# Preparing each delta unit inside the levels of the one before, quarter-chunk filling, and the eight branch gates in a row

## The reference

```python
q = l2_normalize(heads(q)); k = l2_normalize(heads(k)); v = heads(v)
beta = sigmoid(b_in); g = -exp(a_log) * softplus(a_in + dt_bias)
# chunked gated delta rule, 8 heads of 128
decay = exp(where(causal, g[:, None] - g[None, :], -inf))
lower = where(strict, (k*beta @ k.T) * decay, 0)
sol   = triangular_solve(lower + I, [v*beta, k*beta*exp(g)])
intra = (q @ k.T) * decay
...
o = rms_norm(o, norm_w) * silu(z)
y_d = o @ w_dn_out
...
merged = g_a * y_a + g_c * y_c + g_d * y_d
return x + merged @ w_out
```

## Time and profile before

| | |
|---|---|
| median of 3 runs | 2815.61 us (2809.57 to 2818.78) |
| time of the profiled execution | 2811.89 us |
| its span in the profile | 2809.7 us |
| TensorE matmul busy | 2582.6 us, 92% |
| VectorE, ScalarE, GpSimd busy | 44%, 45%, 53% |
| delta units, layer 0 | 380 to 614 us |
| branch gates, layer 0 | from 614 us |

### The profile page before, as it was taken

One profiled execution on the slowest core, in us unless ns is written; L12 is line 12 of the kernel. 1 busy time (PEld: TensorE's weight loads), 2 busy tenths in 40 slices (PEclk: granted clock), 3 DMA queues, 4 the chain that ended last, 5 costly groups with the idle time before them and its releaser, 6 DMA issues.

```text
span 2809.7 us, 42096 instructions
## 1 busy us (share of the span) xinstructions
PE 2582.6 (92%) x16608; PEld 2213.4 (79%) x16608; DVE 1235.8 (44%) x2156; ACT 1266.2 (45%) x2102; POOL 1479.2 (53%) x857
## 2 busy tenths in 40 slices
PE   6998999989899898988989999998999999898997
PEld 6986878879898687887856776776788868688997
DVE  7782743432677273444347532215000126735323
ACT  5455943344545684434453431234233344434543
POOL 6873754337886476343633122564455546373880
PEclk9998999999999899999999999999999999999999
DMA  5442333244444233334331111223222232134554
GB/s 218 180 150 105 119 138 134 106 150 166 179 168 149 97 129 135 132 124 154 139 131 60 46 61 60 75 90 120 79 91 90 93 117 106 61 120 165 180 185 145
DMA packets 50551, 347.62 MB, mean 124 GB/s; under 512 B 5312, under 2 KB 8640, under 8 KB 8896
## 3 DMA queue, kind: packets, MB, share of 16 engines
q1 hardware_dynamic: 47840, 340.31, 33.5%
q10 hardware_dynamic: 2528, 4.72, 0.5%
HBM read 343.96 MB, written 1.05 MB: 123 GB/s over the span
## 4 chain that ended last, share of the span: by engine, by line
PE 78%; DVE 10%; ACT 6%; issue 2%; POOL 1%; DMA 1%; SPq 0%; ACTq 0%; POOLq 0%; DVEq 0%
PE pg L1706 20%; PE pg L1707 19%; PE pg L1708 19%; PE pg L1731 2%; PE ps L1958 2%; PE ps L1846 2%; PE ps L1966 2%; PE ps L1964 1%; DMA ring<-in_w_stream_dram 1%; ACT ring_hi L708 1%; PE ps L2101 1%; PE ps L1827 1%; POOL ring_lo L601 1%; PE ps L2173 1%; PE ps L2082 1%
## 5 line engine op out<-in xcount | busy, mean ns | idle before, releaser
L601 POOL TENSOR_TENSOR ring_lo<-ring,ring_hi 128x1024 fp32r<-128x1024 f32 (+3 forms) x500 | 1169.9, 2353 | 879.8 <-ACT ring_hi L708 879.1
L1706 PE MATMUL pg<-HH,ring_hi 128*128 128x256 f32 (+1 forms) x3360 | 1075.0, 320 | 32.3 <-DVE HL L1201 10.8
L1707 PE MATMUL pg<-HH,ring_lo 128*128 128x256 f32 (+1 forms) x3360 | 1035.2, 308 | 0.0
L1708 PE MATMUL pg<-HL,ring_hi 128*128 128x256 f32 (+1 forms) x3104 | 961.9, 310 | 0.0
L1706 PEld LDWEIGHTS pg<-HH,ring_hi 128*128 128x128 f32 x3360 | 647.5, 193 | 104.7 <-issue 43.0
L1707 PEld LDWEIGHTS pg<-HH,ring_lo 128*128 128x128 f32 x3360 | 648.2, 193 | 38.9 <-issue 10.6
L1708 PEld LDWEIGHTS pg<-HL,ring_hi 128*128 128x128 f32 x3104 | 598.2, 193 | 30.9
L708 ACT ACTIVATE ring_hi<-ring 128x1024 fp32r<-128x1024 f32 (+6 forms) x564 | 556.5, 1002 | 40.8 <-DMA ring<-in_w_stream_dram 29.6
L718 ACT ACTIVATE take<-pg 128x256 f32<-128x256 f32 (+1 forms) x284 | 120.4, 424 | 532.3 <-PE pg L1708 480.8
L1708 PE MATMUL pg<-big_r,ring_hi 128*128 128x256 f32 (+1 forms) x864 | 276.6, 320 | 0.0
L1706 PE MATMUL pg<-big_r,ring_hi 128*128 128x256 f32 (+1 forms) x736 | 242.3, 329 | 9.3 <-DVE big_r L1646 3.1
(11 more groups left out here) (285 smaller groups left out, 3409.8 us busy)
## 6 DMA issues: line engine op xcount, KB each, us to landing
ring<-in_w_stream_dram SPq DMA_DIRECT2D x320, 1024.0 KB, 4.8
hn<-in_consts_dram ACTq DMA_DIRECT2D x2, 1024.0 KB, 5.6
cst<-in_consts_dram SPq DMA_DIRECT2D x1, 1472.0 KB, 19.8
prm<-in_params_dram SPq DMA_DIRECT2D x1, 1110.0 KB, 7.5
X<-in_xT_dram SPq DMA_DIRECT2D x1, 1024.0 KB, 5.8
X<-in_ctxT_dram ACTq DMA_DIRECT2D x1, 1024.0 KB, 7.9
out_dram<-H ACTq DMA_DIRECT2D x1, 1024.0 KB, 4.8
cst<-in_consts_dram SPq DMA_DIRECT2D x1, 768.0 KB, 16.8
```

The costliest lines, as they stand in the source:

```text
L601: pool.tensor_tensor(ring_lo[:, slot, cols], ring[:, slot, cols], ring_hi[:, place * P:(place + n) * P].bitcast(F32), SUB).then_inc(sem(LO ...
L1706: first = pe.matmul(out, a[0], b[0], start=start, stop=False)
L1707: pe.matmul(out, a[1], b[0], start=False, stop=False)
L1708: return first, pe.matmul(out, a[0], b[1], start=False, stop=stop)
```

## The change

- **Units.** The four preparing products of unit u+1, and what VectorE and ScalarE do with them, move into levels 2 to 5 of unit u. All four go one after the other through `ps` bank 0 (unit 0 still uses four banks). `DT`, `LT`, `IN`, `TT`, `QG` and `EXR` get second buffers. The four exps (and the one of `EXR`) of unit u+1 stand on ScalarE behind the second gap of level 2. The turn of the inverse stands behind the last state product of unit u. The keys are turned at level 6, so only four scalings stand between the values' turn and the next product. Two products move to other banks.
- **Filling.** A chunk or row is cut into quarters. The gaps are new, `dz` comes ahead of `az`, and 12.1 of 82.4 gap units lie ahead of unit 0 (`DELTA_START`).
- **Rows.** The row ahead of the attention's head norm runs as a whole before it, and its turn behind the first `dz` chunk. In `delta_gates` the turn moves from right behind its row to behind the small projection.
- **Branch gates.** The eight gate chunks run in a row, with the modulation row after two of them and its turn after three; they are drained into a buffer `DGATE`, the first of them on ScalarE ahead of `hn_root`. Then come the eight odd chunks, and the filter's steps stand one to two chunks apart instead of two to four.

```diff
-GAPS = [0.8, 5, 0.8] + [1, 1.5] * 5 + [0.6, 2, 0.64, 1, 0.8]
+GAPS = [0.4, 1.0] + [1.9, 0.3] * 4 + [1.9, 0.7] + [1.6, 1.1, 1.0, 0.2]
+LAST_GAPS = [0.4, 1.0] + [1.9, 1.0] * 4 + [1.9, 0.7] + [1.6, 1.1, 1.0, 0.9]
+DELTA_START = [4.3, 7.8]
-    return {"modt": 1}.get(name, 2)
+    return {"modt": 1}.get(name, 4)
...
+def branch_gates(l):
+
+    gates = [("d_out", l, i) for i in range(0, 2 * KD, 2)]
+    row, turn = mods(l, "do")
+    return gates[:2] + [row] + gates[2:3] + [turn] + gates[3:]
...
-        FILTER_1 = [0, 4, 8, 12, 14]
+        FILTER_1 = [0, 2, 4, 6, 7]
```

The preparing products, a new function of TensorE (the other two steps, k·k and k·q, wait for `d_lb` and `d_lt`):

```diff
+            def delta_pre(l, u, step):
+
+                i = 4 * l + u
+                dst = ps[:, 0 if u else step, :]
+                if step == 0:
+                    pe.wait_ge(sem("d_ugib"), i + 1)
...
+                if step == 1:
+                    if u:
+                        pe.wait_ge(sem("d_dt"), i + 1)
+                        pe.wait_ge(sem("d_exr"), i + 1)
```

TensorE, level v of unit u, and the last state product:

```diff
                         ins = pe.matmul(ps[:, 1, s], LM[v % 2][:, s], TM[:, s], start=True, stop=True)
                     ins.then_inc(sem("d_x"), 1)
+                    if 2 <= v <= 5 and u < UNITS - 1:
+                        delta_pre(l, u + 1, v - 2)
+                    if v == 6:
...
+                            ins = pe.transpose(ps[:, 0, s], kT(h, c), ident)
+                        ins.then_inc(sem("d_kt"), 1)
                     fill(next(gaps))
...
                     pe.wait_ge(sem("d_xs"), 6 * i + v)
...
                 ins.then_inc(sem("d_v1"), 1)
+                if u < UNITS - 1:
+                    delta_turn(l, u + 1)
                 fill(next(gaps))
```

VectorE, level s of unit u (n is the next unit):

```diff
+                    if n:
+                        if s == 1 and u:
+                            diagonals(l, n)
+                        if s == 2:
+                            pre_decay(l, n)
+                        if s == 3:
+                            pre_beta(l, n)
+                        if s == 4:
+                            pre_keys(l, n)
+                        if s == 5:
+                            pre_inverse(l, n)
+                            pre_queries(l, n)
+                        if s == 6:
+                            dve.wait_ge(sem("d_x"), 6 * i + 5)
+                            level(l, n, 1)
+                            pre_grown(l, n)
+                    if s == 6:
+                        turned_keys(l, u)
```

ScalarE in unit u, and behind the units:

```diff
                 for s in range(1, 7):
                     fill()
                     act.wait_ge(sem("d_x"), 6 * i + s)
                     act.activation(XS, ps[:, 1, :], ACT.Copy).then_inc(sem("d_xs"), 1)
                     fill()
+                    if s == 2 and u < UNITS - 1:
+                        delta_exps(l, u + 1)
...
                 hn_square(DN[:, 0:8, :])
+                gates = branch_gates(l)
+                drain_fill(gates[:1])
                 hn_root(HN_BASE1(l) + DO_N, 2048, 1.0 / P)
-                drain_fill([("d_out", l, 0)])
-                drain_fill(mods(l, "do"))
+                drain_fill(gates[1:6])
```

TensorE around the units:

```diff
-                fill([("part", mods(l, "att")[0])])
+                fill(mods(l, "att"))
                 head_norm(HN_BASE1(l) + ATT_N, 2048)
-                fill(mods(l, "att"))
+                fill(delta_fill(l)[0])
+                for step in range(4):
+                    delta_pre(l, 0, step)
+                fill(delta_fill(l)[1])
+                delta_turn(l, 0)
                 for u in range(UNITS):
                     delta(l, u)
-                fill([("d_out", l, 0)])
+                gates = branch_gates(l)
+                fill(gates[:1])
                 head_norm(HN_BASE1(l) + DO_N, 2048)
-                fill(mods(l, "do"))
-                for i in range(2 * KD):
+                fill(gates[1:])
+                for m in range(KD):
+                    fill([("d_out", l, 2 * m + 1)])
```

More of the change, by code:

```diff
@@ L211, in delta_fill @@
         parts += [("part", x)] * (n_parts(x[0]) - 1) + [x]
-    gaps = [1.08] + (GAPS * UNITS)[1:]
+    parts.insert(4, parts.pop(0))
+    gaps = DELTA_START + GAPS * (UNITS - 1) + LAST_GAPS
     out = [[] for _ in gaps]
@@ L248, in chunk_order @@
         add("dn", 0, 24)
-        add("cz", 0, EARLY_CZ // 2)
-        out += mods(l, "gates")
-        add("cz", EARLY_CZ // 2, EARLY_CZ)
+        row, turn = mods(l, "gates")
+        add("cz", 0, 2)
+        out.append(row)
+        add("cz", 2, 3)
+        out.append(turn)
+        add("cz", 3, EARLY_CZ)
         out += sum(att_fill(l), []) + mods(l, "att") + whole(sum(delta_fill(l), []))
-        add("d_out", 0, 1)
-        out += mods(l, "do")
-        add("d_out", 1, 16)
+        out += branch_gates(l) + [("d_out", l, i) for i in range(1, 2 * KD, 2)]
         add("w_out", 0, 8)
@@ L739, in drain_fill @@
                         drain(CHUNK[name, l, i], CV[:, i, :], ACT.Silu)
+                    elif name == "d_out" and i % 2 == 0:
+                        drain(CHUNK[name, l, i], DGATE[:, i // 2, :], ACT.Sigmoid)
                     elif name in ("cz", "az"):
@@ L865, in delta_gates @@
                 act.activation(EXA, PR("dn_a_log", l * HEADS, HEADS), ACT.Exp).then_inc(sem("exp_a"), 1)
[L866 to L869, removed]
+                row, turn = mods(l, "gates")
+                drain_fill([("cz", l, 1), row, ("cz", l, 2), turn, ("cz", l, 3)])
                 act.wait_ge(sem("abs_a"), l + 1)
@@ L1905, in delta_gates @@
                 head_norm(HN_BASE1(l) + DK_N, 2048)
-                fill([("cz", l, m) for m in range(1, EARLY_CZ // 2)] + mods(l, "gates"))
-                fill([("cz", l, 2)])
+                row, turn = mods(l, "gates")
+                fill([("cz", l, 1), row, ("cz", l, 2)])
                 pe.wait_ge(sem("hn_done"), HN_BASE1(l) + DK_N + 1)
@@ L1925, in delta, with delta_turn @@
+            def delta_turn(l, u):
+                i = 4 * l + u
+                pe.wait_ge(sem("d_tt"), i + 1)
+                if u == 0:
+                    pe.wait_ge(sem("d_exr"), i + 1)
+                for h, c, s in delta_pair(u):
+                    ins = pe.transpose(ps[:, 0, s], TTS[u % 2][:, s], ident)
+                ins.then_inc(sem("d_t0"), 1)
             def delta(l, u):
                 i = 4 * l + u
-                pair = [(2 * u + p // 2, p % 2, slice(p * P, (p + 1) * P)) for p in range(4)]
@@ L1945, in delta @@
-                fill(next(gaps))
-                pe.wait_ge(sem("d_tt"), i + 1)
-                for h, c, s in pair:
-                    ins = pe.transpose(ps[:, 0, s], TT[:, s], ident)
-                ins.then_inc(sem("d_t0"), 1)
+                pair = delta_pair(u)
+                TT, IN, QG = TTS[u % 2], INS[u % 2], QGS[u % 2]
+                gaps = unit_gaps(l, u)
                 for v in range(1, 7):
@@ L1968, in delta @@
                 for h, c, s in pair:
-                    pe.transpose(ps[:, 0, s], kT(h, c), ident)
-                for h, c, s in pair:
                     ins = pe.transpose(ps[:, 1, s], vT(h, c), ident)
-                ins.then_inc(sem("d_kv"), 1)
+                ins.then_inc(sem("d_vt"), 1)
                 fill(next(gaps))
```

223 lines of the change are left out of this document (139 added, 84 removed).

## The result

| | before | after |
|---|---|---|
| median | 2817.2 us (4 runs, 2809.57 to 2823.7) | **2741.75 us** (4 runs, 2739.5 to 2745.33) |
| ratio to before | | 0.9734, 95% interval 0.9706 to 0.9762 |
| profiled execution, its span | 2811.89, 2809.7 us | 2739.78, 2737.8 us |

The change makes the kernel 2.7% faster. The profiled executions differ by 72.1 us. Three marks on TensorE cut each layer: the attention's head norm, the first gate chunk behind the last unit, and the norm behind `w_out`.

What follows compares the result with a forecast made beforehand. TensorE, busy 92% of the span, bounds the kernel. Gains of 31.5 us per layer, twice 63, less 2 for the filter, give 61: 2751 us for the profiled execution, 2755 us as median; range 2728 to 2790 us.

Steps and rivals of the forecast that it cites:

- The inverse's turn: In the units, the three waits at line 1948 go because preparation starts a unit earlier: 8.2 us gained per layer.
- The clock: In the stretch of the units, slow time behind removed waits comes back: 7 of 7.5 us per layer.
- The other waits in the levels: In the units, 9.6 us of other waits per layer become 8 (5 kept, 3 for exps): gain 1.6 us.
- the 3 us for the exps: In level 3, X's copy stands behind the next unit's exps: 1 us of wait in each of three units.
- all is hidden: Rival: no wait left in the levels or the filter, 3.5 us in the delta gates: 2731 us, chance 0.08.
- Ahead of unit 0: Before the attention's head norm, waits for squares and the row's drain shrink, 1.3 us staying: gain 4.4 us per layer.
- Branch gates: Behind the last unit, the turn waits 0.8 us, not 6.25: 6.5 us idle gained, 3 us more from the clock.
- The worst case: In the branch gates, if gate 4's split lands late, 3 us stay.
- Delta gates: The turn's wait of 3.51 us shrinks to 2.7 for GpSimd's split of `cz` 2: gain 0.8 us per layer.
- The filter: In layer 1 alone, closer steps have less cover and wait: a loss of 2 us, range 0 to 9.
- the signs of being wrong: Waits over 1 us at level 3's second products, filter steps or gates' low parts; level waits above 17 us per layer.
- VectorE behind GpSimd: Rival: three masks in level 5 each meet a split, lasting 2.1 us longer: 2779 us; chance 0.17 with another rival.

Runs made afterwards that it cites:

- the doses: The changed kernel with three, or one, further unused exponentials on ScalarE behind each prepared unit's exps: 2756.26 us with three, 2746.06 us with one.
- the early split: The changed kernel with ScalarE and GpSimd making the splits due at `cz` 1 right behind `cz` 0, in the delta gates: 2734.16 us.

## Why the prediction was right, and where it was off

The sign, the places and most sizes held. By its terms, per layer:

- **The inverse's turn, 8.2 us.** Right: no wait is left there. The run with quarters alone keeps 7.4 us, so it is the move that does it.
- **The clock, 7 us.** Right: the stretch runs at 1.00, so all of the 7.5 us came back. TensorE's busy time from head norm to head norm fell by 7.2 us with quarters and by 11.3 with halves: the quarters, which the forecast took to cost nothing, took 4.1 us of it back.
- **The other waits in the levels, a gain of 1.6 us.** This is the term that was mis-sized, by 8.0 us per layer. It measured 9.6: none of the 5 us that I kept and none of the 3 us for the exps came. ScalarE's queue ahead of the copy of X is as long as I added up, but TensorE's work from copy to copy covers it with 0.2, 1.1 and 2.3 us to spare, as the doses show. The 5 us I had kept without a mechanism; of the old waits 2.4 to 3.9 come back when filling is coarser or less. The waits of 0.2 us for VectorE at a level's first product, twelve in layer 0 of the kernel before, are in no list, and the forecast had no term for them. Of the four rivals, "all is hidden" was thus right in the levels and wrong behind them.
- **Ahead of unit 0, 4.4 us.** Right: 5.7 us of waits became 1.1; I had left 1.3.
- **Branch gates, 6.5 and 3 us.** Right in their place: the turn waits 0.74 us (0.8 forecast) at a clock of 1.00. But the stage to the norm won 6.3 us in layer 0, not 9.5. The text took the odd chunks to cost what they did. GpSimd now splits `w_out`'s first chunks between the last merges, so the last low parts come late, and the waits at `w_out`'s start are 3.9 us where one of 1.7 stood. Moving those splits took them to 0.6. Behind these waits the low clock returns (0.50 from 643.2 to 646.5), so that TensorE's busy time in the stage fell by 1.0 us and not by 3. Against that the norm's own wait is 1.3 us shorter. The worst case, a late low part of a gate, did not come in this trace (0.37 us); in four other runs it cost 1.4 to 2.2 us.
- **Delta gates, 0.8 us.** The wait is 2.81 us (2.7 forecast), so the step was right. Up to the first attention product (302.54 us, now 300.20) the stage gained 2.3 us, 1.6 more than this wait shrank by: from 252 to 300 us TensorE is busy for 42.7 us at a clock of 0.84, and was for 44.3 us at 0.80.
- **The filter, a loss of 2 us.** Mis-sized: layer 1 won 5.5 us less than forecast in this stage beyond those 2. One forecast wait of 0 to 3 us came, of 2.59; what it set off, 3.3 us at the low clock in a single product and a slow chunk behind it, I had not counted, though I had counted just that behind every other wait. A wait of over 1 us at a step of the filter was among the signs of being wrong, and that sign came. Taking GpSimd's split away gave 5.6 us back.
- **VectorE behind GpSimd.** The rival had the right mechanism in the wrong place. No wait in the levels comes of it; it decides the filter's pass.

Over both layers the stage of the units gave 16.9 us more than forecast, the stage ahead of it 2.7 more, and the stage behind it 8.7 less. That leaves 10.9 us more than the forecast's 61.

## What to carry to other kernels

A chain that feeds the next round is best begun inside this round, behind second buffers: that took away its own wait and most small waits beside it, while finer filling lost more than it won, because a row cut in four takes as long per piece as one cut in two. Where filling goes inside a level counts as well: the same amount spread evenly cost 5.3 us in layer 0, nearly half of it in waits too short for a list. So look at starts, not only at idle time. When a queue is added up against the time that covers it, let the sum decide: if it fits, count no wait. Count the slow clock behind each new wait as well as behind each old one, and look for the operation of another engine that runs just across a chain with little cover.

## What was not expected of the hardware

- Four of a row's matmuls, 32 columns wide each, take TensorE 1.05 us where eight take 1.06. In quarters the rows of a layer cost 5.2 us more than in halves.
- Each return from a unit's product to a chunk costs TensorE 0.08 us: a first step of 0.20 us against 0.12.
- A VectorE operation with a single source was held by GpSimd's split as those with two are: 2.37 us for 0.28.
- A wait of 2.59 us was followed by a product at 7.02 us for 3.70, at a granted clock of 0.57: the wait cost less than what followed it.
- The small projection, 16 columns wide, falls to the low clock while it runs, with no wait ahead of it or in it: with the early split its steps are 0.11 us until 269.7 and 0.21 from there to its end.
